# Low parts of weight units: from one engine to two, by stage

## The reference, cut to what matters

```
(conv_val, conv_glu, conv_z, dq, dk, dv, dz, dbeta, ddecay,
 aq, ak, av, az, mgate) = split(h @ w_in)
delta branch:  q, k, v = silu(depthwise_conv3(dq, dk, dv)); q, k l2-normalised;
               chunked gated delta rule in both directions; rms_norm * silu(dz)
attention:     difference of two softmaxes over 768 keys, 4 heads; rms_norm * silu(az)
conv branch:   val * sigmoid(glu), depthwise conv of 31 taps, layer_norm, silu * silu(conv_z)
merge:         x + gate * (sum_n sigmoid(mgate_n) * (y_n @ w_branch_n)) @ w_out
modulation:    shift, scale, gate = silu(c) @ w_ada + b_ada   (for c and c_ctx)
```

## Time and profile before

| what | value |
|---|---|
| median of 3 runs | 2073.14 us (2070.95 to 2074.45) |
| profiled execution: its time | 2072.0 us |
| profiled execution: span | 2070.2 us |
| TensorE matmul busy | 1841.0 us (89%), weight loads 1527.5 us |
| VectorE busy | 1076.6 us (52%), 1536 instructions |
| ScalarE busy | 974.0 us (47%), 1300 instructions |
| GpSimd busy | 851.9 us (41%), 638 instructions, 601.3 us of them low parts |
| mean granted clock of TensorE | 0.94 |

### The profile page before, as it was taken

The page is one execution under the profiler, slowest core; times in us unless marked ns, Lnnn a source line. Parts: engine busy times, 40 slices in busy tenths (PEclk is TensorE's granted clock), DMA queues, the critical chain, the costliest instruction groups (busy, mean ns, idle before and its releaser), DMA issues. The chain is left out here.

```text
span 2070.2 us, 27795 instructions
## 1 busy us (share of the span) xinstructions
PE 1841.0 (89%) x11060; PEld 1527.5 (74%) x11060; DVE 1076.6 (52%) x1536; ACT 974.0 (47%) x1300; POOL 851.9 (41%) x638
## 2 busy tenths in 40 slices
PE   6879996999998989878898977989699989788989
PEld 5768886888877777767687865868697767666767
DVE  4656492568665464534123135648759765454122
ACT  6556524255344534533453245563336455444551
POOL 2133335555544343333367212344246534323473
PEclk9989997999999999989998998999899999999999
DMA  7123223412221222213234212224222212112343
GB/s 280 51 68 97 67 92 121 143 42 62 72 72 51 69 67 84 70 49 92 89 107 158 97 56 73 83 89 114 83 72 61 75 58 64 54 51 72 97 125 130
DMA packets 76415, 178.87 MB, mean 86 GB/s; under 512 B 6464, under 2 KB 29312, under 8 KB 76160
## 3 DMA queue, kind: packets, MB, share of 16 engines
q1 hardware_dynamic: 34272, 122.46, 19.5%
q10 hardware_dynamic: 42016, 54.63, 7.8%
HBM read 156.00 MB, written 21.07 MB: 86 GB/s over the span
## 5 line engine op out<-in xcount | busy, mean ns | idle before, releaser
L1879 POOL TENSOR_TENSOR wLs<-raw,wHs 128x512 fp32r<-128x512 f32 x420 | 601.3, 1455 | 832.0 <-ACT wHs L830 831.9
L465 PE MATMUL banks<-hH,wHs 128*128 128x512 f32 x1984 | 606.0, 367 | 60.6 <-DVE hL L433 20.4
L465 PE MATMUL banks<-hL,wHs 128*128 128x512 f32 x1984 | 586.8, 358 | 0.0
L465 PE MATMUL banks<-hH,wLs 128*128 128x512 f32 x1984 | 585.4, 357 | 0.0
L465 PEld LDWEIGHTS banks<-hH,wHs 128*128 128x128 f32 x1984 | 330.9, 194 | 135.0 <-issue 26.4
L465 PEld LDWEIGHTS banks<-hL,wHs 128*128 128x128 f32 x1984 | 329.7, 194 | 57.2 <-issue 2.6
L465 PEld LDWEIGHTS banks<-hH,wLs 128*128 128x128 f32 x1984 | 328.4, 193 | 55.8
L830 ACT ACTIVATE wHs<-raw 128x1024 fp32r<-128x1024 f32 x210 | 220.4, 1053 | 260.8 <-DMA raw<-wstream 260.6
L1449 DVE SCALAR_TENSOR_TENSOR acc<-padc,vecs,acc 128x783 f32<-128x783 f32 (+1 forms) x240 | 296.4, 1291 | 0.0
L819 ACT ACT_TABLE_LOAD x183 | 234.8, 1283 | 29.2 <-issue 11.9
L864 ACT ACTIVATE Pa<-banks,stat 128x768 f32<-128x768 f32 (+1 forms) x80 | 64.5, 812 | 134.1 <-DVE stat L1409 132.1
(11 more groups left out here) (241 smaller groups left out, 2430.4 us busy)
## 6 DMA issues: line engine op xcount, KB each, us to landing
raw<-wstream SPq DMA_DIRECT2D x210, 512.0 KB, 3.6
araw<-wstream SPq DMA_DIRECT2D x16, 512.0 KB, 12.5
E<-g_rows ACTq DMA_DIRECT2D x16, 384.0 KB, 6.6
egb<-eg_rows ACTq DMA_DIRECT2D x20, 256.0 KB, 4.1
inb<-intra_rows ACTq DMA_DIRECT2D x20, 256.0 KB, 4.6
parked_logits<-sg ACTq DMA_DIRECT2D x13, 384.0 KB, 4.1
xs<-xT SPq DMA_DIRECT2D x8, 384.0 KB, 11.4
intra_rows<-E ACTq DMA_DIRECT2D x8, 384.0 KB, 3.1
```

What stands on the lines that cost most here:

```text
L465: last = pe.matmul(out[:, a:b], w, m[:, kt, a:b], start=(kt == 0 and j == 0), stop=(kt == kts - 1 and j == 2))
L1879: ins = pool.tensor_tensor(wL[w % RING][:, o:o + 512], raw[w % RING][:, o:o + 512], wH[w % RING][:, o:o + 512].bitcast(F32), ALU.subtract)
```

## The change

A function names the units whose low parts VectorE makes: gb, dk, dv, dq, cz, branch2, branch0, wout and the ada units of layer 0. GpSimd skips them in its `ahead`; it keeps val, glu, dz, aq, ak, av, az, the gates, branch1 and the ada units of layer 1. VectorE gets a function `low`, called at the start of each item's work with a reach of RING - 1: up to two units beyond the item's own. It waits for the high part and subtracts all 1024 columns in one instruction.

```diff
+def low_on_vector(u):
+
+    return u[0] in ("gb", "dk", "dv", "dq", "cz", "branch2", "branch0", "wout") or u[0] == "ada" and u[1] == 0
...
             added = set()
+            done_lo = [0]
+
+            def low(u, n):
+
+                while done_lo[0] < min(WIDX[u] + n, len(UNITS)):
+                    w = done_lo[0]
+                    v = UNITS[w]
+                    done_lo[0] += 1
+                    if not low_on_vector(v):
+                        continue
+                    dve.wait_ge(*done("hi", v))
+                    dve.tensor_tensor(wL[w % RING][:, :], raw[w % RING][:, :], wH[w % RING][:, :].bitcast(F32),
+                                      ALU.subtract).then_inc(*tick("dve", "lo", v))
...
+                    if l == 0 and m == 6:
+                        low(UNITS[0], RING - 1)
+                    for u in units_of(it):
+                        low(u, RING - 1)
...
                 elif k == "gb":
+                    low(units_of(it)[0], RING - 1)
...
+                    low((kind, l, h), RING - 1)
                     w0 = V_DW + 3 * (NT * ("dq", "dk", "dv").index(kind) + h)
                     dve.wait_ge(*done("read", (kind, l, h), 0))
...
+                    low(("val", l, t), RING - 1)
+                    low(("glu", l, t), RING - 1)
...
+                    low(("branch%d" % n_, l, p), RING - 1)
...
                 elif k in ("gate", "qunit", "vunit"):
+                    low(units_of(it)[0], RING - 1)
                     conv(l, 1)
+                elif k in ("park", "leafpark", "z"):
+                    low(units_of(it)[0], RING - 1)
...
+                    low(("az", l, h), RING - 1)
...
                     t, u = it[2], ("wout", l, it[2])
+                    low(u, RING - 1)
...
                     w = done_lo[0]
                     v = UNITS[w]
                     done_lo[0] += 1
+                    if low_on_vector(v):
+                        continue
                     pool.wait_ge(*done("hi", v))
                     for o in (0, 512):
```

## The result

The changed kernel takes **2036.5 us** (median of 4 runs, 2032.6 to 2041.7) against 2072.6 (4 runs, 2070.95 to 2074.45): a ratio of 0.983, interval 0.980 to 0.985. That is 36 us less, where I had forecast 19. The range I gave began at 2042, so the result lies outside it, on the quick side. The profiled execution took 2035.0 us, its span is 2033.2 us.

A forecast was written before the change was run, and what follows sets the result against it. TensorE's waits bound the kernel, with in-order GpSimd's low parts delaying VectorE on chains TensorE waits for. Terms 9.5 + 2.5 + 4.7 + 0.9 - 2.9 + 4.4 = 19.1 us gave 2054.0 us; 8-in-10 range 2042 to 2072.

The forecast's parts named there:

- delta preparation: dq taps to `pad`: 1.9 us off the chain at each of five `pad` waits, 9.5 us; bounds 0 and 18.0.
- the `sqd` wait: First head of the preparations: TensorE's wait for squares shrinks, but counts as no gain, since TensorE then waits at `pad`.
- The bound of 18.0 us: Upper bound of the delta preparation term: all five `pad` waits of TensorE together.
- Late merges: GpSimd's chain before branch0 gets shorter: 4.7 us in layer 1, 0.9 in layer 0; bounds for both 0 and 9.7.
- ada: Layer 0: TensorE's waits for ada low parts shrink, 2 x 1.28 = 2.5 us; bounds 0 and 5.
- Start of the projections: VectorE's low part of wout 2 delays the first `hL`: cost 2.0 us in layer 0, 0.9 in layer 1, -2.9.
- The other order: Start of layer 0's output projection: were GpSimd's add to start first, the loss would be some 2 us more.
- the middle of the output projection: TensorE is never late for these low parts and VectorE waits for TensorE in each item: nothing gained.
- Clock: Half-clock stretches behind two `pad` waits and layer 1's branch 0 wait may go: 4.4 us; bounds 0 and 8.
- A: Chains where ScalarE is second engine: relief passed on only in part, 2067 us; chance 0.23.
- B: VectorE units hold off GpSimd's adds or squares as GpSimd held off taps, eating the gain: 2072 us; chance 0.08.
- C: Low parts ahead of VectorE's taps are not covered by idle time: slower, 2097 us, or 2083; chance 0.09.

The follow-up runs named there:

- the changed kernel's other profile: The changed kernel run once more without edits, in the same rounds as three other kernels: 2034.6 us, ratio 0.9831.
- the two reordered ones: Kernel before, GpSimd's low part at the dq item put behind the squares (2062.0 us), or later z items' low part put behind `acc` x `rsc` (2067.4 us).
- one pair too many: Changed kernel with all val and glu units of layer 1 also on VectorE and wout 2's low part behind the eight `hL`: 2035.0 us, ratio 0.983.
- a ghost that reads: Changed kernel plus two unused GpSimd subtractions, reading constants, for each of the preparations' 26 units: 2060.8 us, ratio 0.9954.
- a ghost that only fills: Changed kernel plus five unused GpSimd fills, reading nothing, for each of the preparations' 26 units: 2043.2 us, ratio 0.9874.
- the one with the z items reordered: Kernel before, with GpSimd making the low part of later z items behind `acc` x `rsc`, ahead of `yL`: 2067.4 us, ratio 0.998.

## Why the prediction was right or wrong

**The direction and the mechanism were right; the step that failed is the price of delta preparation.** That term was "5 x 1.9 = 9.5 us", one chain (dq taps to `pad`) at five places, with the `sqd` wait put at nothing. The preparations brought 18.6 us when moved alone and 22.0 in the table above. What the runs showed in its place:

- *The `pad` waits themselves fell by 9.4 us, almost the term, but not by 1.9 each.* In order they lost 0.4, 1.9, 0.6, 2.3 and 4.2 us. That the sum came out is luck.
- *The `sqd` waits counted.* I had called the shrinking wait in the first head "no gain of its own, since TensorE then waits at `pad` instead". It shrank by 2.6 us in layer 0 and by 3.4 in layer 1, and the `pad` wait behind it did not grow (4.21 us before, 3.83 after; 5.25 and 4.68). So these 6.1 us were kept. The bound of 18.0 us, the sum of the `pad` waits, was too low for the same reason: the `sqd` waits (16.4 us) belonged to it.
- *More than the dq taps lies on the path of the first heads.* The dk and dv taps stand ahead of the dq taps there, and they lost 1.3 us each in both layers (4.0 to 2.7 us from first start to last end). This is the second tap of dk in layer 1, before and after:

```profile
1253.61 1.93 DVE L1554 SCALAR_TENSOR_TENSOR c<-pad,vecs,c 128x769 f32<-128x769 f32 x1
```
```profile
1240.30 1.02 DVE L1579 SCALAR_TENSOR_TENSOR c<-pad,vecs,c 128x769 f32<-128x769 f32 x1
```

- *The width.* I wrote that undisturbed taps would take 2.8 us, and worked with 768 columns, while the very rows that I compared with, are 512 wide. They take 2.06 us: 2.6 us less and not 1.9, at the three places of layer 1.

**Late merges: 4.7 + 0.9 forecast, about 7 in the traces, 10 by the ratio.** TensorE's wait in layer 1 went from 6.83 to 1.72 us, as said ("near 2"). But the working behind it was wrong, and the size is luck. I let the two adds end at 1982.9 without the low part, although GpSimd is at `yL` until 1982.5 (timeline of the kernel before):

```profile
1981.21 1.29 POOL L1887 TENSOR_TENSOR yL<-zt,yH 128x512 fp32r<-128x512 f32 x1 [2.38 <-ACT yH L1265]
```

Behind it the adds end at 1985.0 at best, so this step was worth 2.5 us and not 4.5. In the trace the last round is even 0.5 us longer (10.1 for 9.7). The gain came from the rounds ahead of it, for which I had put 0.7: the first `acc` x `rsc` comes 3.3 us earlier in the changed kernel (offset to the kernel before 33.3 us, 30.1 where attention ends), and the three rounds together are 1.9 us shorter (32.5 for 34.4). The 3 us between traces and ratio are no more than the scatter seen in layer 1's last head; what they are stays open.

**ada: 2.5 forecast, 4.4 to 5 measured.** The waits went from 6.01 to 4.70 us and from 2.50 to 1.35, 2.5 us together, exactly the term. The rest can be the leaf chain beside it, for which I had written that TensorE does not wait: its wait there, just ahead of the product at 349.4, went from 4.22 to 2.82 us. In the changed kernel's other profile it is 4.78, though, so this part is not shown.

**Start of the projections: -2.9 forecast, and there it was.** Layer 0's first step waits 4.75 us against 2.01 + 1.14, layer 1's 3.68 against 2.36 + 0.66: 1.6 and 0.7 us. Putting the low part behind the eight `hL` gave 2.4 us back in layer 0. The other order, for which I had named some 2 us more, did not occur: VectorE's low part starts at 1113.79, GpSimd's last add at 1113.95. What I missed is the other side: "the middle of the output projection ... nothing". The rest of the projections makes up what their start loses, so that wout alone is not 2.9 us slower.

**Clock: 4.4 forecast.** All three stretches that I had named were granted 1.00 after, as this answer of the trace (same columns as above) shows: layer 1 head 2 (0.58 before), branch 0 (0.50 before), layer 0 head 2. In the two first heads, where TensorE still waits at `pad`, it comes back at 0.50.

```profile
1325.80:1329.80 4.00, 4.00 (x23) 3.46 (x23) 3.91 (x3) 3.95 (x5) 2.15 (x2) 1.00 0.93 212
1957.47:1961.07 3.60, 3.60 (x16) 2.91 (x17) 2.76 (x2) 2.77 (x4) 3.39 (x2) 1.00 0.76 240
186.40:190.40 4.00, 4.00 (x23) 3.49 (x24) 3.90 (x3) 3.95 (x5) 2.09 (x2) 1.00 0.61 172
119.34:123.34 4.00, 4.00 (x13) 3.42 (x14) 2.60 (x3) 3.95 (x5) 0.00 (x0) 0.50 0.01 4
```

Where a `pad` wait vanished, the gain of the clock can be read right behind it: 1.5 us in layer 0, head 2, and 1.4 in layer 1, head 2; at branch 0 it is 1.7. That is 4.6 us, close to the term. But the third is not sure to come with the short wait: in layer 0 TensorE was granted 0.54 over 3.6 us behind a wait of 1.80 us ahead of branch 0.

TensorE's whole busy time fell by 12.2 us, almost three times the term. Part of that is no effect of the change: the kernel with wout alone has TensorE busy for 1835.0 us instead of 1841.0, and the two reordered ones that are 8 and 3.5 us quicker have 1831.4 and 1831.0, against 1828.8 of the changed kernel. So beyond the 4.6 us of the three places the profiles do not tell what is the clock's.

**Rivals.** A (relief passed on in part) was wrong: it was passed on in full, and there was more of it than I had counted. B, the even exchange between engines that share access, was wrong for this list of units; the caution that I quoted for it (the Trainium skill, Perfetto Trace Analysis, "Optimizing Scalar/DVE Operations": offloading between the two might not help) did not hold for the change. It is nearer to the truth for the kernel with all units on VectorE, though there the waits name VectorE's order, not the port, as what cost. C's mechanism, a low part on VectorE that has no cover, is real: 41.1 us of waits with all units, 12.39 us in one place with one pair too many, but not at the taps.

## What to carry to other kernels

A helper instruction on a slower engine costs by its time in the queue (most where it waits for an input that comes later than what stands behind it) and by the slowing of the neighbour with which it shares access to SBUF; a ghost that reads and a ghost that only fills tell the parts roughly apart, while a change of order moves both at once, since it also moves the disturbance. Choose its engine by stage, by which one stands idle ahead of its next due work, and keep it from standing behind a long in-order chain. When a chain is shortened, price it by the very shapes in its rows, count every step of it that the neighbour slowed, and every wait ahead of the one you look at. Before you let a step start earlier, look up what its engine is doing at that time.

## What the runs showed of the hardware

- A VectorE instruction with two SBUF inputs (128x512) takes 0.75 us alone and beside GpSimd's fills, 1.66 to 1.83 us beside GpSimd's reading subtractions; a scaling with one input takes 0.49 alone, 0.92 beside fills, 1.13 beside subtractions. I had not expected the fills to touch the scaling.
- GpSimd pays as well: the square of 128x768 takes 1.47 us when the taps are over and 1.92 beside them, and the adds of 128x512 into `mT` took 2.20 us beside VectorE's low part, 1.28 without.
- After a wait of 3.83 us at `pad` in the first head TensorE was granted 0.50 (1.2 GHz) over the next 4 us, although it was busy all of that time, while after a wait of 1.72 us ahead of branch 0 it was granted 1.00 (2.4 GHz). The length of the wait alone does not settle it: at the same product of layer 1's last head the kernel before waits 3.45 us and is granted 0.50 over the next 3.6 us, the one with the z items reordered waits 3.50 us and is granted 1.00.
